# Which operand is loaded and which is streamed in the inner layer of the block compression

## The reference

```
def compress_blocks(kv, pe, w1, w2):
    ...
    sub = kv.reshape(b, g, n_sub, CMP_STRIDE, d)
    blocks = jnp.concatenate([sub[:, :, r:r + n_cmp] for r in range(ratio)], axis=3)
    blocks = (blocks + pe).reshape(b, g, n_cmp, CMP_LEN * d)
    return jax.nn.silu(blocks @ w1) @ w2
```

## Time and profile before

| | us |
|---|---|
| median of 3 runs | 1802.73 |
| lowest and highest run | 1802.36, 1802.81 |
| the profiled execution, its own time | 1802.82 |
| its span, from first to last instruction | 1801.0 |
| PE busy in the span | 1780.4 |
| DVE, ACT, POOL busy | 915.3, 792.0, 637.2 |

### The profile page before, as it was taken

The page is one execution under the profiler, slowest core; times in us unless marked ns, Lnnn a source line. Parts: engine busy times, 40 slices in busy tenths (PEclk is TensorE's granted clock), DMA queues, the critical chain, the costliest instruction groups (busy, mean ns, idle before and its releaser), DMA issues.

```text
span 1801.0 us, 24814 instructions
## 1 busy us (share of the span) xinstructions
PE 1780.4 (99%) x9830; PEld 1433.8 (80%) x9830; DVE 915.3 (51%) x2045; ACT 792.0 (44%) x1713; POOL 637.2 (35%) x390
## 2 busy tenths in 40 slices
PE   9999999999999999999999999999999999999997
PEld 6787876788988888889876788888877777887676
DVE  4558588553211101134778267674744243567764
ACT  5324355454331222234567445553354344446662
POOL 4534421154444453434322433223342324332222
PEclk9999999999999999999999999999999999999999
DMA  5322311143433232324222332113322322431211
GB/s 171 99 71 71 95 47 36 32 149 103 127 94 106 84 115 82 94 78 115 62 45 71 94 97 74 56 60 84 116 71 58 82 71 78 108 68 35 59 58 70
DMA packets 215029, 147.91 MB, mean 82 GB/s; under 512 B 51953, under 2 KB 197377, under 8 KB 214914
## 3 DMA queue, kind: packets, MB, share of 16 engines
q1 hardware_dynamic: 210592, 136.84, 27.1%
q10 hardware_dynamic: 4322, 9.50, 1.6%
HBM read 144.22 MB, written 2.10 MB: 81 GB/s over the span
## 4 chain that ended last, share of the span: by engine, by line
PE 93%; DVE 5%; ACT 1%; issue 0%; DMA 0%; POOL 0%; DVEq 0%; ACTq 0%
PE PS L392 25%; PE PS L394 24%; PE PS L393 24%; PE PS L480 6%; PE PS L541 6%; PE PS L565 4%; PE PS L733 1%; ACT X L1072 1%; DVE PS L1541 1%; DVE X L1544 1%; PE PS L954 1%; PE PS L933 1%; DVE PS L1560 1%; PE PS L754 0%; DMA row<-in_norm_mix 0%
## 5 line engine op out<-in xcount | busy, mean ns | idle before, releaser
L2134 POOL TENSOR_TENSOR Wl<-Wr,Wh 128x1024 fp32r<-128x1024 f32 (+5 forms) x385 | 636.5, 1672 | 1129.7 <-ACT Wh L1013 1129.2
L392 PE MATMUL PS<-XTl,Wh 128*128 128x512 f32 (+1 forms) x1096 | 412.8, 377 | 1.0 <-DVE OBl L1576 0.8
L394 PE MATMUL PS<-XTh,Wh 128*128 128x512 f32 (+1 forms) x1096 | 408.1, 372 | 0.0
L393 PE MATMUL PS<-XTh,Wl 128*128 128x512 f32 (+1 forms) x1096 | 408.0, 372 | 0.0
L1013 ACT CAST Wh<-Wr 128x1024 fp32r<-128x1024 f32 (+5 forms) x292 | 268.3, 938 | 183.2 <-PE PS L394 136.6
L392 PEld LDWEIGHTS PS<-XTl,Wh 128*128 128x128 f32 x1096 | 206.6, 188 | 45.6 <-issue 9.7
L394 PEld LDWEIGHTS PS<-XTh,Wh 128*128 128x128 f32 x1096 | 206.4, 188 | 36.3
L393 PEld LDWEIGHTS PS<-XTh,Wl 128*128 128x128 f32 x1096 | 206.6, 188 | 34.7
L392 PE MATMUL PS<-Wl,XTh 128*128 128x512 f32 (+2 forms) x608 | 227.2, 374 | 0.6 <-POOL Wl L2134 0.6
L394 PE MATMUL PS<-Wh,XTh 128*128 128x512 f32 (+2 forms) x608 | 224.1, 369 | 0.0
L393 PE MATMUL PS<-Wh,XTl 128*128 128x512 f32 (+2 forms) x608 | 223.9, 368 | 0.0
(11 more groups left out here) (324 smaller groups left out, 2552.5 us busy)
## 6 DMA issues: line engine op xcount, KB each, us to landing
Wr<-in_w_in SPq DMA_DIRECT2D x38, 512.0 KB, 3.8
Wr<-in_fox_w_in SPq DMA_DIRECT2D x32, 512.0 KB, 4.1
Wr<-in_w_ffn_gate SPq DMA_DIRECT2D x22, 512.0 KB, 3.9
Wr<-in_w_ffn_up SPq DMA_DIRECT2D x22, 512.0 KB, 3.9
Wr<-in_w_ffn_down SPq DMA_DIRECT2D x22, 512.0 KB, 3.6
Wr<-in_swa_w_in SPq DMA_DIRECT2D x20, 512.0 KB, 3.9
Wr<-in_mla_w_in SPq DMA_DIRECT2D x16, 512.0 KB, 4.1
Wr<-in_mla_w_out SPq DMA_DIRECT2D x16, 512.0 KB, 3.5
```

What stands on the lines that cost most here:

```text
L392: pe.matmul(o, l[0], r[1], start=start, stop=False)
L393: pe.matmul(o, l[1], r[0], start=False, stop=False)
L394: return pe.matmul(o, l[0], r[0], start=False, stop=stop)
L2134: ins = raw.tensor_tensor(l[:, cs], r[:, cs], h[:, cs].bitcast(F), sub)
```

## The change

In `mm3` of the four compression jobs the operands change places: a 128x128 slice of the weights is loaded, and 70 columns of `KX`, eight floats apart, are streamed. The result is 128 hidden units by 70 columns, as DVE wants it. So `HR`, ACT's two copies into it, PE's two transposes and their two banks go away, and DVE reads the first bank. `KF` and `KX` get 568 columns in place of 560.

```diff
-                        KX = [splits(c3, "KX", [128, 560]) for _ in range(2)]
-                        KF = alloc(c3, "KF", [128, 560])
+                        KX = [splits(c3, "KX", [128, 568]) for _ in range(2)]
+                        KF = alloc(c3, "KF", [128, 568])
...
-                        lhs = [KX[j][u][:, l0 + l:l0 + l + 545:8] for u in range(2)]
-                        ins = mm3(PS[b][0:69, 0:128], lhs, part(i, l, 128), l0 + l == 0, l0 + l == 15)
+                        blocks = [KX[j][u][:, l0 + l:l0 + l + 553:8] for u in range(2)]
+                        ins = mm3(PS[b][:, 0:70], part(i, l, 128), blocks, l0 + l == 0, l0 + l == 15)
                     if l0 == 8:
                         ins.then_inc(*done(psum_full, "ch", j))
                         used[i] = psum_full.now()
-                        give(b, (by_act, ("ch", j)))
+                        give(b, (by_dve, ("hc", j, 1)))
...
                 elif name in ("ca", "cb"):
-                    j = int(name == "cb")
-                    b = take(("ct", j))
-                    e.wait_ge(by_act.at("ch", j), *free(b))
-                    transposes(b, [(HR[j][0:69, :], 0)], ("ct", j), psum_full)
-                    give(b, (by_dve, ("hc", j, 1)))
+                    pass
...
-                elif name in ("ck8", "cv8"):
-                    j = int(name == "cv8")
-                    after(psum_full, "ch", j)
-                    high(HR[j][0:69, :], bank["ch", j][0:69, 0:128], "ch", j)
...
-                        weights(psum_full, "ct", j)
+                        weights(psum_full, "ch", j)
                         e.wait_ge(by_dve.at("hc_in", j, g))
...
-                    e.wait_ge(psum_full.at("ct", j))
+                    e.wait_ge(psum_full.at("ch", j))
                     for g in range(2):
-                        x, b = 2 * j + g, bank["ct", j]
+                        x, b = 2 * j + g, bank["ch", j]
```

More of the change, by code:

```diff
@@ L214, in program @@
                     CW2 = [alloc(c2, "W2", [128, 64]) for _ in range(2)]
-                    HR, tn = [alloc(c2, "HR", [128, 128]) for _ in range(2)], alloc(c2, "tn", [128, 2, 64])
+                    tn = alloc(c2, "tn", [128, 2, 64])
                     HB, HC, HTT = alloc(c2, "HB", [128, 4]), alloc(c2, "HC", [128, 4, 32]), alloc(c2, "HT", [128, 4, 32])
```

## The result

The changed kernel takes 1809.45 us (median of 6 runs, 1809.06 to 1810.13), the kernel before on the same chip 1802.58 (1802.13 to 1802.90). The ratio is 1.0039, with an interval of 1.0029 to 1.0049: 6.9 us slower. The forecast was 1804.0 with a range up to 1806.2, so it missed on the slow side. The mean granted clock of TensorE is 0.992 to 0.994 in its six runs; the runs of the kernel before that stand beside the experiments have 0.998 or 0.999. The profiled execution took 1809.51 us, its span is 1807.7.

The account below looks back on a forecast made before the run. PE, busy 99% of the span, was taken as the bound. Streams -1.2, m2's late cast +1.8 and level 9's wait +0.7 gave +1.3 us on 1802.82, 1804.1; as median 1804.0 us, range 1801.2 to 1806.2.

Parts of the forecast that it names:

- The pace of the stream: Compression's 96 matmuls on PE: from 0.133 to 0.120 us each with contiguous loads, 1.2 us saved.
- Rivals (2) and (3): Strided stream bounds the compression: at the load's rate, nothing saved, 1805.2 (0.22); or far costlier, about 1815 (0.08).
- The late cast of m2: ACT casts m2 behind the keys' two HT; PE stands about 2.0 us, m2 starts 1.8 us later.
- The wait at level 9: POOL's m4 operation holds DVE's first L1730 until 211.6, so PE waits 0.7 us for its bank.
- Rival (4): At level 9 DVE's L1730 isn't held by POOL, so PE doesn't wait: 1803.3 us, chance 0.15.
- Rival (5), the clock: PE's 2 us stand before m2 lets its clock fall to half speed: 1807 us, chance 0.04.
- What is removed: PE's two transposes, each delaying the next job 0.09 us, and ACT's copies, lying in waits: worth nothing beside the pace.
- Within 0.2%: Whole kernel's time differs from no change by less than can be measured, 3.6 us: chance 0.86.
- slower: Whole kernel measurably slower, above 1806.3 us, by rivals (3), (5) and a tail of (2): chance 0.13.

Follow-up runs that it names:

- contig280_casts: Changed kernel with ACT's casts back in their old places, streaming 280 contiguous (wrong) columns in place of 70 strided: 1801.64 us, one run.
- cols140: Changed kernel, casts still late, streaming 140 columns four floats apart (every second one ballast) in place of 70 eight apart: 1804.37 us.
- cols140_parts4: cols140 with POOL making m4's low part in four short operations in place of one: 1804.65 us, one run.
- casts_back: Changed kernel with places for ACT's casts restored where its copies to HR stood, so m2 and m3 are cast early: 1808.03 us.
- contig140_casts: casts_back streaming 140 contiguous columns of KX, the wrong blocks, in place of 70 strided: 1799.95 us, one run.
- packed_copies_casts: casts_back with KF reordered in the copies from PSUM, so 70 contiguous columns are streamed twice over: 1800.28 us, ratio 0.9989.
- mix_casts: casts_back with high-times-high matmuls streaming the 70 columns twice, the two low-part ones 70: 1800.35 to 1800.50 us in four executions, 1805.37 to 1809.59 in eight.
- cols140_casts: cols140 with the early casts of casts_back: 1802.02 us, ratio 0.9998.
- old64: Kernel before, in its own operand order, streaming 64 of 128 hidden units in all slices but the first and last: 1804.78 us, one run.
- contig70_casts: casts_back with the 70 streamed columns contiguous (wrong blocks) in place of eight floats apart: 1810.05 us, one run.

## Why the prediction was wrong, point by point

- **The pace of the stream**: forecast 0.120 us a matmul, measured 0.112 while the clock was 1.00, below even its lower bound (0.114). The term was mis-sized by the wrong nearest row: 0.120 holds for 256 streamed columns and 0.129 for 280 (`contig280_casts`), while 70 and 140 contiguous ones both go at 0.112, so there the load alone is the bound. At full clock the saving is 2 x (7.56 - 6.60) = 1.9 us and not 1.2.
- **Rivals (2) and (3)**, a strided stream as the bound: wrong. "Doubled, as the load is" was right, 0.79 ns a column. The price of the load, 1.7 ns, doesn't hold for the stream.
- **The late cast of m2**: forecast 1.8 us later than before, 8.57 - 6.82 = 1.75 at full clock (`cols140`). In the changed kernel 0.93, since the slow clock made the distance from level 7, on which the cast hangs, to level 8 longer, and so swallowed a part of the wait.
- **The wait at level 9**: forecast 0.7 us, measured 0.73, by the mechanism named: L1722 held for 1.55 us. The trace and the Trainium skill's "SBUF — State Buffer", section "Who interferes with whom", agree, and `cols140_parts4` shows the hold to follow the length of POOL's operation. That the number fits so well is partly luck, for the working has a slip: 211.6 + 0.84 is 212.4 and not 212.6, which leaves 0.5 us. PE began m2 210.46 - 207.60 = 2.86 us behind POOL's start and not 3.02, and so stood before level 9 that much earlier. Rival (4) is out. The pieces cv8, m1, m3 and m4 came in time, as said.
- **Rival (5), the clock**: this is the step that failed. It was put at 0.04, and only for PE's stand of 2 us; in the sum the clock has no term, which takes it at 1.00 throughout. The prediction looked at the clock as something that a wait endangers, and asked of the streams only how fast they issue. The clock fell before any wait, in the first stream, with PE busy throughout. What it costs: with early casts 1808.03 - 1799.95 = 8.1 us (`casts_back` against the one run of `contig140_casts`; against `packed_copies_casts`, 7.8, as between the two groups of `mix_casts`). With the late ones an estimate of 1799.95 + 2.35 = 1802.3 without the fall (2.35 being what the casts cost between `cols140` and `cols140_casts`), against 1809.45, makes 7.1 us. That is the whole loss, by this estimate: without it the change would have gained about as much in the streams as it lost in the two waits. The Trainium skill, "TensorE: Matmul & The Clock Gate", section "HAM oscillation — how this bites in real kernels", tells of the clock lost in idle gaps; here it was lost with PE listed busy throughout.
- **What is removed**: the transposes give 6.84 - 6.76 = 0.08 us, as said. DVE found the result ready.
- "Within 0.2%" was given 0.86 and "slower" 0.13. The sum itself was good: `cols140`, in which the clock holds and both waits stand, takes 1804.37, by luck partly, since its ballast takes away most of the streams' gain (1.9 us at full clock, of which it keeps 7.56 - 7.46 + 7.56 - 7.48 = 0.2).

What stays open is what the chip compares when it lowers the clock. In these runs the clock fell with 64 columns streamed beside 69 strided loaded ones and with 70 beside 128; it held with 128 beside the 69 and with 140 or 280 beside 128; a mixture of 70 and 140 did either. They don't show whether columns, matmul time or something else is counted. Nor do they show why it came back where it did.

## What to carry to other kernels

When operands change places, count the columns that are streamed for each load, before and after: a run of matmuls bound by their loads can run into half of TensorE's clock without a single wait in the list, as here with 64 and 70 columns, and the work behind it pays too. If an order would gain but for that, try ballast that hides behind the load (here 140 contiguous columns at 0.112 us), and put the reordering where a strided read from PSUM is made anyway. Together that was worth 2.1 us here (1800.28 beside 1802.40). And a wait taken out of an engine's list takes out what was issued in it: here two places of casts, worth 1.4 us in the changed kernel and 2.35 at full clock.

## What the runs showed of the hardware that was not expected

- The granted clock fell from 1.00 to 0.50 with PE listed busy for the whole of the stretch, in four kernels with 64 or 70 streamed columns, and stayed there for 14 to 20 us (about 186.6 to 200.2 in `old64`, 184.8 to 205.3 in `contig70_casts`).
- One program (`mix_casts`) held the clock in 4 of 12 executions and lost it in 8, with up to 9.2 us between them.
- At half clock a pace that 128 contiguous loaded columns set goes from 0.112 to 0.213 us. One that 69 strided loaded columns set stays at 0.131 (`old64`), so what sets that pace doesn't slow with TensorE's clock (one run).
- A stride about doubles the price of a streamed column, from 0.4 to 0.79 ns, and two neighbours at a time don't help (0.129 us for 70 pairs, 0.129 for 140 single columns, 0.112 for 140 contiguous ones).
- Rearranged splits in SBUF took ACT 1.30 us in place of 0.67 and DVE 1.35 in place of 0.75, while the copies from PSUM that read and write in the new order took 0.38 and 0.42 us in place of 0.37 and 0.42.
